# Rounded output products in the first block, and another order of the last mixer's gate chunks

## The chip, the core and the metric

The kernel is one program on one core of a Trainium2 chip. The metric is the device time of one execution in microseconds (us), as the median of some executions. The engines have queues of their own that run in program order: TensorE (PE, matrix products), VectorE (DVE), ScalarE (ACT), GpSimd (POOL), and SyncE (SP), which starts the weight transfers. They wait for one another through semaphores.

## What is computed

Two small transformer stacks, one after the other, over 256 latent tokens of width 1024 (and 256 context tokens in the first layer). Only the parts that the change touches are shown.

```python
# first block, layer 0: pooling beside a gated scan, then one output product
o = rmsnorm(o_sum, onorm_g).reshape(Bn, Ln, HG_WIDTH).astype(g.dtype) * jax.nn.silu(g)
return jnp.concatenate([multiscale_pool(u, pool_w, pool_scale), o], axis=-1) @ w_out
...
x = x + g1 * rmsnorm(y_lat, norm_g[l, 1])
f_lat = swiglu(rmsnorm(x, norm_g[l, 2]) * (1.0 + sc2) + sh2, ffn_w_in[l], ffn_w_out[l])
...
# second block, last mixer (mixer 3): gated delta rule, z is its output gate
lmat = jnp.where(strict, jnp.einsum('nbhid,nbhjd->nbhij', kb, k) * decay, 0.0)
amat = lmat + jnp.eye(CHUNK, dtype=f32)
u = lax.linalg.triangular_solve(amat, v * beta[..., None], left_side=True, lower=True, unit_diagonal=True)
...
o = (o * jax.nn.silu(z.astype(jnp.float32))).astype(x.dtype)
return o.reshape(b, s, C_WIDTH) @ w_out
```

## The kernel before

All weights come as one stream of chunks of 1 MB (128 partitions x 2048 float32) into a ring of six slots; SP loads a slot again once PE has signalled that its chunk is multiplied. The order of the stages is a fixed list, and the order of the work on each engine is the order in which its function is written.

**Split products.** Nearly all products are made from rounded numbers. ACT rounds a chunk into a place of its own (the high part, L494), DVE writes the difference over the ring slot (the low part, L500), and PE adds three products: high by high, high by low, low by high. Inputs are split in the same way (`X_HI` by ACT, `X_LO` by DVE at L521). A product from unsplit float32 numbers is one instruction in the program and two records in the trace.

**The tail of the first mixer (mixer 0).** PE mixes the four heads (L871) into banks 0 to 3 and sums their squares (L876); ACT makes the inverse roots (L953, L955); DVE scales each head out of its bank and multiplies it by its gate (L1077, L1080). Then comes the output product for 4 tiles (2 blocks of 128 tokens by 2 halves of 512 features) of each of two streams, latent and context, unsplit, from `pe_tokens` (L656): 16 products of 128x256 a tile. PE's order is: four latent tiles, one context tile, the latent tokens turned back (`pe_turn_tokens`, L673), one context tile, the sum of squares for the next norm (`pe_norm`, L231), two context tiles. DVE and ACT meanwhile take token statistics (`dve_rms_tokens`, L693 to L702; `act_rms_tokens`, L681 to L685), add the turned tokens to the residual (L711), and make the input of the feed-forward (`dve_scale_output`, L624, L627, L521, with ACT's L484). The feed-forward `ffn0_lat` starts with `pe_chunks_as_features_come` (L299): 32 products of the high weights by the high input, 32 of the low weights, 32 by the low input. It waits until the first half of the context tokens has left banks 4 and 5.

**The same pattern twice more.** After mixer 1 (`mix1_post`, then `ffn1_lat`) and after `ffn1_lat` (then `ffn2`, turned by `pe_turn_both`, L1484) tokens are measured, scaled, turned and added, and there PE has nothing to put beside it. In `dve_add_turned` the additions alternate with the low parts of the next input.

**Mixer 3.** PE multiplies 16 chunks; 12 to 15 are the gate z (48 products of 128x256 each, L286 to L288). After z chunk 12 come eight sums of squares over heads (`head_sums`, L2028), four row spreads (`spread`, L2035), then for each of 8 heads four products (`head_products`, L2043, L2046), with z chunks 13 and 14 between them. DVE's chain over the heads is `decays` (L2377 to L2384), `triangles` (L2390, L2391), `query_decays` (L2394) and `rest_of_head` (L2398, L2399); it holds the difference of chunk 15 between heads 1 and 2. Then six levels of a triangular inverse follow. In a level PE makes `product` (L2098) after DVE's mask (L2420), and four `increments3` groups (L2111, L2116), which DVE adds in (L2445, L2449). z chunk 15 is cut in four parts of 12 products (`last_z_part`, L2076 to L2078), one ahead of each of levels 2 to 5.

## Time and profile before

| what | us |
|---|---|
| median of 3 runs | 2217.38 |
| the runs | 2217.25, 2217.38, 2224.48 |
| the profiled execution, own time | 2223.95 |
| its span in the profile | 2222.0 |
| PE busy in the span | 2151.3 (97%) |
| DVE busy | 1401.9 (63%) |
| ACT busy | 986.8 (44%) |
| POOL busy | 173.4 (8%) |

A time in the trace counts from the start of the span. The engine that is nearly always busy is PE, so the reading looks for the some 70 us in which PE stands still, and for stretches in which its granted clock is one half.

### The profile page before, as it was taken

The numbers are of one execution on the slowest core, as the hardware profiler recorded it, in microseconds if no ns is written. First come the engines' busy times: TensorE is split into PE (matmuls) and PEld (weight loads), VectorE is DVE, ScalarE is ACT, GpSimd is POOL, SyncE is SP. The second block draws the span as 40 slices with busy tenths as digits, with TensorE's granted clock in tenths as the row PEclk, the third lists the DMA queues.
The fourth block names the chain that finished last, engine by engine and source line by source line (L and its number), as shares of the span: only waits on it lengthen the run. The fifth ranks groups of instructions, "written<-read, shape, count | busy, mean of one in ns | idle before, by whom it ended". The sixth has DMA issues, their size and how long they took to land. (4 is left out here: it accounts for less than half of the span.)

```text
span 2222.0 us, 32315 instructions
## 1 busy us (share of the span) xinstructions
PE 2151.3 (97%) x13514; PEld 1851.3 (83%) x13514; DVE 1401.9 (63%) x1602; ACT 986.8 (44%) x1114; POOL 173.4 (8%) x94
## 2 busy tenths in 40 slices
PE   6999999999999999999999999999999999999999
PEld 4887788888888857888888898888988897878888
DVE  4367845666766456656665678656665687566665
ACT  3312333444544234444444555445444565254444
POOL 0065600000000000000100011000100012001000
PEclk8999999999999999999999999999999998999999
DMA  8227913455455412355555533555455442124552
GB/s 334 106 100 295 412 74 131 165 191 192 160 189 189 169 72 76 138 192 189 200 189 189 189 133 142 189 189 189 167 191 190 170 166 100 36 91 163 191 192 79
DMA packets 52609, 373.28 MB, mean 168 GB/s; under 512 B 5792, under 2 KB 6816, under 8 KB 7968
## 3 DMA queue, kind: packets, MB, share of 16 engines
q1 hardware_dynamic: 51632, 367.71, 44.9%
q0 software_dynamic: 880, 4.19, 0.5%
q8 instruction: 71, 1.16, 0.2%
q14 instruction: 26, 0.21, 0.0%
HBM read 370.84 MB, written 1.05 MB: 167 GB/s over the span
## 5 line engine op out<-in xcount | busy, mean ns | idle before, releaser
L500 DVE TENSOR_TENSOR ring_r<-ring,AR_r 128x2048 fp32r<-128x2048 f32 x286 | 655.3, 2298 | 267.3 <-ACT AR_r L494 267.1
L494 ACT ACTIVATE AR_r<-ring 128x2048 fp32r<-128x2048 f32 x286 | 545.0, 1911 | 326.2 <-PE PS L397 195.0
L376 PE MATMUL PS<-AR_r 128*128 128x512 f32 x2240 | 533.2, 390 | 0.0
L376 PEld LDWEIGHTS PS<-AR_r 128*128 128x128 f32 x2240 | 415.6, 188 | 83.1
L380 PEld LDWEIGHTS PS<-AR_r,ring_r 128*128 128x128 f32 x2240 | 287.2, 191 | 10.9
L380 PE MATMUL PS<-AR_r,ring_r 128*128 128x256 f32 x2240 | 290.6, 283 | 0.0
L541 ACT ACTIVATE AR<-PS 128x512 f32<-128x512 f32 x140 | 83.7, 598 | 418.6 <-PE PS L380 418.6
L395 PE MATMUL PS<-AR_r 128*128 128x512 f32 x616 | 241.4, 392 | 0.0
L396 PE MATMUL PS<-ring_r,AR_r 128*128 128x512 f32 x616 | 241.1, 391 | 0.0
L397 PE MATMUL PS<-AR_r 128*128 128x512 f32 x616 | 240.4, 390 | 0.0
L397 PEld LDWEIGHTS PS<-AR_r 128*128 128x128 f32 x616 | 116.0, 188 | 24.7
L603 DVE TENSOR_TENSOR AR<-AR,PS 128x512 f32<-128x512 f32 x70 | 48.1, 688 | 138.9 <-ACT AR L541 138.9
L395 PEld LDWEIGHTS PS<-AR_r 128*128 128x128 f32 x616 | 116.4, 189 | 22.4
L396 PEld LDWEIGHTS PS<-ring_r,AR_r 128*128 128x128 f32 x616 | 116.4, 189 | 21.5
L580 DVE TENSOR_TENSOR AR<-AR,PS 128x512 f32<-128x512 f32 x70 | 48.1, 688 | 95.3 <-ACT AR L541 95.3
L286 PE MATMUL PS<-AR_r 128*128 128x256 f32 x352 | 101.6, 289 | 0.7 <-DVE ring_r L500 0.7
L287 PE MATMUL PS<-AR_r 128*128 128x256 f32 x352 | 99.8, 284 | 0.0
L288 PE MATMUL PS<-AR_r,ring_r 128*128 128x256 f32 x352 | 99.7, 283 | 0.0
L299 PE MATMUL PS<-AR_r 128*128 128x256 f32 x640 | 83.3, 287 | 8.0 <-ACT AR_r L484 4.5
L299 PEld LDWEIGHTS PS<-AR_r 128*128 128x128 f32 x640 | 79.4, 193 | 10.8 <-issue 5.1
L1395 POOL TENSOR_SCALAR X<-X 128x512 f32<-128x512 f32 x24 | 47.6, 2000 | 440.5 <-DVE AR_r L521 440.4
L286 PEld LDWEIGHTS PS<-AR_r 128*128 128x128 f32 x352 | 67.7, 192 | 2.8 <-issue 1.8
(394 smaller groups left out, 2927.2 us busy)
## 6 DMA issues: line engine op xcount, KB each, us to landing
ring<-stream SPq DMA_DIRECT2D x346, 1024.0 KB, 4.8
X<-xt SPq DMA_DIRECT2D x1, 2048.0 KB, 9.0
AR<-bias POOLq DMA_DIRECT2D x1, 1536.0 KB, 6.5
AR<-pt POOLq DMA_DIRECT2D x2, 512.0 KB, 4.5
out<-X SPq DMA_DIRECT2D x4, 256.0 KB, 2.1
AR<-invc SPq DMA_DIRECT2D x1, 512.0 KB, 15.3
X<-negl POOLq DMA_DIRECT2D x1, 512.0 KB, 6.3
H<-wax POOLq DMA_DIRECT2D x1, 512.0 KB, 7.2
```

The costliest lines, as they stand in the source:

```text
L286: pe.matmul(o, w_hi, X_HI[:, k, :], start=(k == 0), stop=False)
L287: pe.matmul(o, w_hi, X_LO[:, k, :], start=False, stop=False)
L288: ins = pe.matmul(o, w_lo, X_HI[:, k, :], start=False, stop=(k == DT - 1))
L299: ins = pe.matmul(PS[:, bank, j * T:(j + 1) * T], w, x[:, k, :], start=(first and j == 0), stop=last, skip_group_check=True)
L376: pe.matmul(PS[:, (6, 4)[half] + j, :], block(w_hi_of(tag, i + half), j, k), X_PARTS[:, k, :], start=(k == 0), stop=False, skip_group_chec ...
L380: ins = pe.matmul(PS[:, (6, 4)[half] + j, 0:T], block(RING_R[:, n % SLOTS, :], j, k), X_HI[:, k, :], start=False, stop=(k == DT - 1), skip ...
L395: pe.matmul(o, G_HI[:, d, f, ts], w_hi, start=False, stop=False, skip_group_check=True)
L396: pe.matmul(o, G_HI[:, d, f, ts], w_lo, start=False, stop=False, skip_group_check=True)
L397: ins = pe.matmul(o, G_LO[:, d, f, ts], w_hi, start=False, stop=(last and f == 1), skip_group_check=True)
L494: act.activation(w_hi_of(tag, i), ring[:, n % SLOTS, :], ACT.Identity).then_inc(split_hi, 1)
L500: dve.tensor_tensor(RING_R[:, n % SLOTS, :], ring[:, n % SLOTS, :], w_hi_of(tag, i), ALU.subtract).then_inc(split_lo, 1)
L541: act.activation(out[:, it % 2, :].rearrange("p (j t) -> p j t", j=2), PS[:, bank:bank + 2, T:T2], ACT.Identity).then_inc(ffn_low, 1)
```

## The change

It has five parts.

1. Mixer 0's output product is split like the others: its chunks hold 256 input features by all 1024 outputs (`chunks_out`), ACT rounds four chunks, DVE makes four differences, the inputs are split too (`POOL_HI`, `SQ_R`, `CAT0_LO`), and PE runs chunk by chunk over all four tiles. Its order: four latent chunks, context chunk 0, the turn, context chunks 1 and 2, the norm's sum, context chunk 3.
2. `dve_scale_output` makes its four multiplications by the inverse root first. This is in all five places that use it.
3. Token statistics and turns: `first_early` scales the first token block before the last statistic (context tokens of mixer 0, `ffn1_lat`); `apart` and `pe_turn_both` let PE turn what is ready instead of waiting for all; `dve_add_turned` makes all additions first, and the difference of `ffn2`'s chunk 1 moves behind them.
4. `pe_chunks_as_features_come` waits for the low weights of each of its two chunks apart.
5. In mixer 3, ACT and DVE split chunk 15 ahead of the norms of the heads; z chunk 13 is cut in two halves, z chunk 15 goes whole between the products of heads 5 and 6, and the level loop holds no z part. PE waits for ACT's logarithms instead of the exponentials before it writes those banks again.

```diff
-SPLIT_OUTS = ('mix1_out', 'mix2_out', 'mix3_out')
+SPLIT_OUTS = ('mix0_out', 'mix1_out', 'mix2_out', 'mix3_out')
...
             for i in chunks:
                 pe.wait_ge(split_lo, SPLIT_BASE[tag] + i + 1)
-            for k in range(DT):
-                products(k, True, X_HI)
+                for k in range(DT):
+                    products(k, True, X_HI, of=(i,))
...
+            for q in range(GROUPS):
+                dve.tensor_tensor(SQ[:, pair(q), cols], src[:, pair(q)], r, ALU.mult).then_inc(S["scaled"], S.mark("scaled", (tag, q)))
             for q in range(GROUPS + 1):
                 if q < GROUPS:
-                    dve.tensor_tensor(SQ[:, pair(q), cols], src[:, pair(q)], r, ALU.mult).then_inc(S["scaled"], S.mark("scaled", (tag, q)))
                     dve.wait_ge(S["scaled"], S.at("scaled", (tag, q)))
...
+                for k in (*range(4, DT), *range(4)) if apart and t == 0 else range(DT):
+                    if apart and k == 0:
+                        pe.wait_ge(S["normed"], S.at("normed", (tag, t)))
+                    if apart and k == 4:
+                        pe.wait_ge(S["token_high"], S.at("token_high", (tag, t)))
...
+            stats(0, 0)
+            stats(0, 1)
+            gather(0)
+            stats(1, 0)
+            if first_early:
+                scale(0)
+            stats(1, 1)
+            gather(1)
+            if not first_early:
+                scale(0)
+            scale(1)
...
+            if nxt:
+                dve_split_chunk(dve, nxt, 1)
+            dve.wait_ge(order.sem, order.n)
             dve.wait_ge(S["residual"], S.at("residual", (tag, GROUPS - 1)))
+            if nxt:
+                dve_split_input(dve, nxt, X[:, :, c])
...
-            pe_tokens(pe, "mix0_out", ctx, CAT0, 0, 0, 0, 4, False)
+            def out_chunk(i, key):
+
+                if key == lat:
+                    pe.wait_ge(split_lo, SPLIT_BASE["mix0_out"] + i + 1)
+                    pe.wait_ge(S["mixer_low"], S.at("mixer_low", ("mix0", i)))
+                for t in range(2):
+                    for h in range(2):
+                        first = T + t * P if key == lat else t * P
+                        if i == 0 and key == lat:
+                            pe.wait_ge(S["mixer_output"], S.at("mixer_output", ("mix0 taken", 2 * t + h)))
...
+            for i in range(4):
+                out_chunk(i, lat)
+            pe.wait_ge(S["o_rinv"], S.at("o_rinv", HEADS - 1))
+            out_chunk(0, ctx)
             pe_turn_tokens(pe, lat, TOK1[0], LOW)
-            pe_tokens(pe, "mix0_out", ctx, CAT0, 0, 0, 1, 5, False)
+            out_chunk(1, ctx)
+            out_chunk(2, ctx)
             pe_norm(pe, ("ffn0_pre", 0), LAT, 0)
-            for h in range(2):
-                pe_tokens(pe, "mix0_out", ctx, CAT0, 0, 1, h, 6 + h, True)
+            out_chunk(3, ctx)
...
+            act_split_chunk(act, "mix0_out", 2, free=START["mix0_out"])
+            for h in range(HEADS):
+                act.wait_ge(S["mixer_output"], S.at("mixer_output", (0, h)))
+                act.activation(SQ_R[:, h, :], GS[:, h, :], ACT.Identity).then_inc(S["x_hi"], S.mark("x_hi", ("mix0_out", 2 + h)))
+            act_split_chunk(act, "mix0_out", 3, free=START["mix0_out"])
...
+            for i in range(2):
+                dve_split_chunk(dve, "mix0_out", i)
+            dve.wait_ge(S["mixed"], S.at("mixed", HEADS - 1))
+            for q in range(2):
+                dve.wait_ge(S["x_hi"], S.at("x_hi", ("mix0_out", q)))
+                dve.tensor_tensor(CAT0_LO[:, pair(q), :], CAT0[:, pair(q), :], POOL_HI[:, pair(q), :], ALU.subtract).then_inc(
+                    S["mixer_low"], S.mark("mixer_low", ("mix0", q)))
...
-            pe_turn_tokens(pe, "mix1_post", TOK1[0], HIGH)
+            pe_turn_tokens(pe, "mix1_post", TOK1[0], HIGH, apart=True)
...
                     if u < 4:
-                        pe.wait_ge(S["head_rinv"], S.at("head_rinv", ("delta", 4 + j)))
+                        pe.wait_ge(S["head_rinv"], S.at("head_rinv", ("log", 4 + j)))
...
             head_sums((4, 5, 6, 7))
+            z_half(13, 0)
             head_sums((0, 1, 2, 3))
-            for h in range(4):
+            for h in range(2):
                 spread(h)
+            z_half(13, 1)
             for h in range(0, 2):
                 head_products(h)
-            z_chunk(13)
+                spread(h + 2)
...
             for h in range(4, 6):
                 head_products(h)
                 spread(h + 2)
+            z_chunk(15)
             for h in range(6, 8):
                 head_products(h)
...
             for lv in range(INNER):
                 first_bank = 0 if lv else 2
-                if lv >= 2:
-                    last_z_part(lv - 2)
...
             for i in range(1, 13):
-                if i < 12:
-                    act_split_chunk(act, "mix3_in", i + 3)
+                act_split_chunk(act, "mix3_in", i + 3)
...
+            dve_split_chunk(dve, "mix3_in", 15)
             for u in (4, 5, 6, 7, 0, 1, 2, 3):
                 dve.wait_ge(S["head_rinv"], S.at("head_rinv", ("delta", u)))
...
-            for i in range(2):
-                dve_split_chunk(dve, "ffn2", i)
-            dve_rms_tokens(dve, order, "ffn1_lat", 0, LOW, TOK1[0], need_tokens(dve, "ffn1_lat", "ffn1_lat", FFN_LAST))
+            dve_split_chunk(dve, "ffn2", 0)
+            dve_rms_tokens(dve, order, "ffn1_lat", 0, LOW, TOK1[0], need_tokens(dve, "ffn1_lat", "ffn1_lat", FFN_LAST), first_early=True)
```

PE at the end of mixer 0, before: the row of the four head sums, the 80 unsplit products, the turn, and on to the feed-forward (L299).

```order
L876 MATMUL PS<-SQ,CO 128x512 x4
L656 MATMUL PS<-ring,AR 128x256 x80
L673 MATMUL PS<-CO,AR 128x128 x16
L656 MATMUL PS<-ring,AR 128x256 x16
L231 MATMUL PS<-SQ,CO 128x256 x8
L656 MATMUL PS<-ring,AR 128x256 x32
L299 MATMUL PS<-AR_r 128x256 x32
```

And now, around the sum for the norm (L231); the L916 rows are the split products, three terms in turn.

```order
L916 MATMUL PS<-ring_r,SQ_r 128x512
L916 MATMUL PS<-AR_r,H_r 128x512
L231 MATMUL PS<-SQ,CO 128x256 x8
L916 MATMUL PS<-AR_r,SQ_r 128x512
L916 MATMUL PS<-ring_r,SQ_r 128x512
L916 MATMUL PS<-AR_r,H_r 128x512
```

The work behind the norm's sum has gone from 32 unsplit products of 256 columns to one chunk, 24 split products of 512 columns; what stands ahead of it has gone from 96 unsplit products to 168 split ones.

DVE where it makes the feed-forward's input and then takes the context tokens' statistics, before:

```order
L624 TENSOR_TENSOR SQ<-X,RI 128x2x256
L627 TENSOR_SCALAR H<-SQ,GV 128x256 x2
L624 TENSOR_TENSOR SQ<-X,RI 128x2x256
L627 TENSOR_SCALAR H<-SQ,GV 128x256 x2
L521 TENSOR_TENSOR AR_r<-H,AR_r 128x2x256
L624 TENSOR_TENSOR SQ<-X,RI 128x2x256
```

and now:

```order
L623 TENSOR_TENSOR SQ<-X,RI 128x2x256 x4
L628 TENSOR_SCALAR H<-SQ,GV 128x256 x4
L521 TENSOR_TENSOR AR_r<-H,AR_r 128x2x256
L628 TENSOR_SCALAR H<-SQ,GV 128x256 x2
L521 TENSOR_TENSOR AR_r<-H,AR_r 128x2x256
L628 TENSOR_SCALAR H<-SQ,GV 128x256 x2
L521 TENSOR_TENSOR AR_r<-H,AR_r 128x2x256 x2
L697 BN_STATS TMP<-PS 128x6 x2
L702 BN_AGGR TMP<-TMP 128x2
L705 SCALAR_TENSOR_TENSOR TMP<-TMP 128x1
L697 BN_STATS TMP<-PS 128x6
L711 TENSOR_SCALAR AR<-PS,TMP 128x512
```

The four multiplications stand in a row ahead of the rest, and the first block's scaling (L711) has moved ahead of the last statistic.

PE in mixer 3, before, from the last product of z chunk 12 to the first of z chunk 13:

```order
L288 MATMUL PS<-AR_r,ring_r 128x256
L2028 MATMUL PS<-SQ,CO 128x512 x8
L2035 MATMUL PS<-AR,CO 128x512 x4
L2043 MATMUL PS<-AR 128x128 x2
L2046 MATMUL PS<-AR 128x128 x2
L2043 MATMUL PS<-AR 128x128 x2
L2046 MATMUL PS<-AR 128x128 x2
L286 MATMUL PS<-AR_r 128x256
```

and now, from the last product of z chunk 13's second half through heads 0 to 2 (L2114 and L2117 are the head products, L2106 the spreads):

```order
L2129 MATMUL PS<-AR_r,ring_r 128x256
L2114 MATMUL PS<-AR 128x128 x2
L2117 MATMUL PS<-AR 128x128 x2
L2106 MATMUL PS<-AR,CO 128x512
L2114 MATMUL PS<-AR 128x128 x2
L2117 MATMUL PS<-AR 128x128 x2
L2106 MATMUL PS<-AR,CO 128x512
L2114 MATMUL PS<-AR 128x128 x2
L2117 MATMUL PS<-AR 128x128 x2
L2106 MATMUL PS<-AR,CO 128x512
```

z chunk 13 has moved ahead of the head products, and spreads stand between them.

## Rows read from the trace of the kernel before

**Rows 1.** The page, busy time of each engine.

```profile
PE 2151.3 (97%) x13514; PEld 1851.3 (83%) x13514; DVE 1401.9 (63%) x1602; ACT 986.8 (44%) x1114; POOL 173.4 (8%) x94
```

**Rows 2.** Timeline of mixer 1's split output products; then page groups of the weight splits.

```profile
869.79 0.39 PE L1217 MATMUL PS<-AR_r 128*128 128x512 f32 x1
...
878.40 0.39 PE L1217 MATMUL PS<-AR_r,H_r 128*128 128x512 f32 x1
...
L500 DVE TENSOR_TENSOR ring_r<-ring,AR_r 128x2048 fp32r<-128x2048 f32 x286 | 655.3, 2298 | 267.3 <-ACT AR_r L494 267.1
L494 ACT ACTIVATE AR_r<-ring 128x2048 fp32r<-128x2048 f32 x286 | 545.0, 1911 | 326.2 <-PE PS L397 195.0
```

**Rows 3.** Timeline of PE, end of mixer 0: start, duration, instruction, [idle before].

```profile
306.19 31.78 PE L656 MATMUL PS<-ring,AR 128*128 128x256 f32 x146 [0.69 <-DVE AR L1080]
...
346.46 3.62 PE L231 MATMUL PS<-SQ,CO 128*128 128x256 f32 x16
349.92 13.98 PE L656 MATMUL PS<-ring,AR 128*128 128x256 f32 x64
365.85 1.34 PE L299 MATMUL PS<-AR_r 128*128 128x256 f32 x9 [1.95 <-DVE AR L702]
```

**Rows 4.** Timeline of DVE and ACT at the same place.

```profile
300.50 0.75 DVE L1077 SCALAR_TENSOR_TENSOR SQ<-PS,SM,SQ 128x512 f32<-128x512 f32 x1 [11.55 <-ACT SQ L955]
...
351.14 0.69 DVE L624 TENSOR_TENSOR SQ<-X,RI 128x512 f32<-128x512 f32 x1 [8.81 <-ACT RI L461]
...
359.05 1.29 DVE L693 BATCH_NORM_STATS2 TMP<-PS 128x6 f32<-128x512 f32 x2
...
361.43 0.69 ACT L685 ACTIVATE AR<-PS,TMP 128x512 f32<-128x512 f32 x1
```

**Rows 5.** Timeline of PE between mixer 1 and its feed-forward.

```profile
881.63 3.32 PE L673 MATMUL PS<-CO,AR 128*128 128x128 f32 x16 [2.84 <-DVE AR L702]
...
892.38 2.50 PE L299 MATMUL PS<-AR_r 128*128 128x256 f32 x16 [3.02 <-ACT AR_r L484]
...
899.05 5.10 PE L299 MATMUL PS<-AR_r,ring_r 128*128 128x256 f32 x32
903.99 4.00 PE L299 MATMUL PS<-AR_r 128*128 128x256 f32 x32
```

**Rows 6.** Timeline of DVE, then PE, between `ffn1_lat` and `ffn2`.

```profile
1076.69 2.29 DVE L500 TENSOR_TENSOR ring_r<-ring,AR_r 128x2048 fp32r<-128x2048 f32 x1 [1.32 <-ACT AR_r L494]
...
1084.69 1.66 DVE L711 SCALAR_TENSOR_TENSOR X<-PS,GV,X 128x256 f32<-128x256 f32 x4 [0.95 <-PE PS L1484]
...
1094.90 4.00 PE L299 MATMUL PS<-AR_r 128*128 128x256 f32 x32
```

**Rows 7.** Stretches of mixer 3: length, busy times, then granted clock, DMA share, GB/s.

```profile
1866.70:1873.10 6.40, 6.37 (x8) 2.14 (x8) 5.67 (x12) 5.33 (x12) 0.00 (x0) 0.56 0.00 0
...
1887.10:1893.10 6.00, 6.00 (x51) 6.00 (x51) 3.28 (x10) 1.31 (x4) 0.00 (x0) 1.00 0.03 11
...
1906.00:1911.50 5.50, 4.86 (x72) 4.33 (x70) 2.74 (x5) 2.33 (x6) 0.00 (x0) 0.50 0.01 3
```

**Rows 8.** Timeline of DVE over mixer 3's heads, then PE's first level product.

```profile
1866.71 2.50 DVE L2366 SCALAR_TENSOR_TENSOR AR<-AR,SQ 128x512 f32<-128x512 f32 x4 [3.96 <-ACT SQ L2234]
...
1875.29 0.28 DVE L2390 TENSOR_TENSOR AR<-AR,PS 64x128 f32<-64x128 f32 x1 [2.20 <-PE PS L2046]
...
1876.91 2.27 DVE L500 TENSOR_TENSOR ring_r<-ring,AR_r 128x2048 fp32r<-128x2048 f32 x1
...
1894.11 0.28 DVE L2390 TENSOR_TENSOR AR<-AR,PS 64x128 f32<-64x128 f32 x1 [3.56 <-PE PS L2046]
...
1903.58 0.62 PE L2098 MATMUL PS<-CO,SQ 64*64 64x64 f32 x14 [2.87 <-DVE SQ L2420]
```

**Rows 9.** Timeline of mixer 3, level 4: DVE's two masks and PE's product.

```profile
1932.28 1.28 DVE L2420 TENSOR_TENSOR SQ<-AR,X 128x512 f32<-128x512 f32 x2
...
1933.18 2.08 PE L2098 MATMUL PS<-AR,SQ 64*64 64x64 f32 x64
```

143 lines of the change are left out of this document (76 added, 67 removed).

## The prediction

> **What bounds the kernel now.** I read the page's busy times first. PE is busy for 2151.3 of 2222.0 us [rows 1], so what an edit is worth is what it takes off PE's queue, or off the 70.7 us in which PE stands still. Next I read the timeline of PE for its idle gaps in the places that the diff touches, then the timelines of DVE and ACT there, for what ends each gap. Last came the granted clock of the stretches in mixer 3, since an idle PE is often followed by a stretch at the lower of the two levels. In the rows the reader should look for three kinds of place: PE full (the output products of mixer 0), PE waiting for a chain through DVE and ACT (the two joints around `ffn1_lat`, the heads of mixer 3), and PE filled with other work just as long as such a chain (the levels of mixer 3).
>
> **Mixer 0: the products.** The unsplit products cost 31.78 us for 146 records, that is 73 products at 0.435 us each [rows 3]. Split products of 512 columns start 38 intervals in 878.40 - 869.79 us, 0.227 us apart [rows 2]. A stream has 64 unsplit or 96 split products, so 27.9 us become 21.8 us.
>
> **Mixer 0: up to the norm.** Ahead of the norm's sum PE had the latent products and two context tiles, 96 x 0.435 = 41.8 us. Now it has 168 x 0.227 = 38.1 us, 3.7 us less. The latent products also stopped for the scaled heads before: one stop of 0.69 us stands in front of 306.19 [rows 3], and with the short ones at their start I count 1.5 us. Now the first chunk needs only the pooled half and the emptied banks. A tile is 6 x 0.227 = 1.36 us, about the pace at which DVE empties the banks, so little of this wait comes back. The norm's sum should end 5.2 us earlier, near 344.7 instead of 349.9.
>
> **Mixer 0: what hides the splits.** They add four ACT passes of 1.91 us and four DVE passes of 2.30 us [rows 2], and the parts of the inputs. DVE sits idle for 11.55 us before 300.50 [rows 4]; two of its passes (4.6 us) and the pooled halves (some 2.5 us, an estimate from half a pass each) fit there. The other two come between the heads' scaling and 314 us or so, while PE has latent chunks of 5.4 us to run; the last is wanted only when chunk 3 is due, near 318. I put these at nothing. If the cover were gone, PE would wait for one DVE pass, 2.3 us, up to two.
>
> **Mixer 0: from the norm to the feed-forward.** Here the bound changes hands. Before, 14.0 us of PE work and a stop of 1.95 us followed the norm's sum, 15.9 us in all [rows 3]. Now PE has only one chunk, 5.4 us, and then waits for DVE. DVE begins the modulation 1.2 us after the sum, is done after 7.9 us (351.14 to 359.05), and the first block's tokens are ready 3.1 us later (361.43 + 0.69 against 359.05), provided that the scaling no longer queues behind the last statistic, which `first_early` sees to [rows 4]. That makes 12.3 us. The feed-forward starts 5.2 + 3.6 = 8.8 us earlier, with a PE gap of 6.9 us in front instead of 1.95. The four multiplications in a row cost DVE nothing more. A gap that long should cost clock: after 2.87 us of idle PE ran at 0.50 for 5.5 us in mixer 3 [rows 7, 8]. I charge 3 us at half speed, 1.5 us, with bounds 0 and 2.8. Sum: -7.3 us.
>
> **After mixer 1.** PE waits 2.84 us and then turns 16 blocks in 3.32 us, at half clock [rows 5]; DVE's additions need ten of them. With `apart`, eight are done in the gap and two after it, so the additions start some 1.8 us earlier. Then the feed-forward's first 32 products follow the high input. They take from 892.38 to 899.05, 6.7 us, because the input comes at DVE's pace; with all multiplications first, ACT alone sets it, four groups at about 1.1 us, then one group of products: 4.3 us. That is 2.4 us more. The next 32 took 5.10 us against 4.00 for the same count at full clock [rows 5], so one stretch of half clock is in this and I leave it in. Sum: -4.2 us, bounds -2 and -5.5.
>
> **Before `ffn2`.** DVE's pass on chunk 1 ends at 1078.98 and only then come the statistics [rows 6], though the first tile's products were done some 2.8 us before. Without that pass, the first statistics start early, the end of the chain is set by the last tile, and the additions start at about 1083.3 instead of 1084.69. Additions in a row give ACT the high input sooner. Chunk 1's difference then ends near 1088.9, in time for its low weights because part 4 lets chunk 0's go first. The last 32 products start near 1092.8 instead of 1094.90. Sum: -2.1 us, bounds 0 and -3.
>
> **Mixer 3: the heads.** DVE's chain from the head norms to the first mask is what PE waits for at 1903.58 (2.87 us idle) [rows 8]. Three delays leave it. The last head norms come 1.3 us earlier: PE no longer idles between the two groups of sums, which gives 1.9 us and more at full clock, less the rounding of chunk 15 that now stands ahead of them on ACT. The wait of 2.20 us for the first head's product goes, since DVE finds it done. The difference of chunk 15, 2.27 us, leaves the middle of the chain for a place where DVE is idle. One delay grows: DVE waited 3.56 us behind z chunk 14; now it waits about 1 us behind chunk 14 and 3.4 us behind chunk 15, each 6.0 us of PE work [rows 7]. Sum: -1.3 - 2.2 - 2.3 + 0.9 = -4.9, and head 7's tail some -0.4: -5.3 us.
>
> **Mixer 3: the levels.** The four z parts are 6 us of PE work, but they cover a DVE chain of the same length. In level 4 the first mask is ready at half of 1.28 us after 1932.28, that is 1932.92; PE's product starts at 1933.18 [rows 9]. Without the part it could start 0.15 us sooner. So four levels give back 0.6 us, not 6, and PE idles about 1.5 us in each. Sum of mixer 3: -5.9 us, bounds -9 (half-clock stretches at 1866.7 and 1906 gone as well) and +2.
>
> **A rule that speaks against this.** The rows show half clock after an idle of 2.87 us [rows 7, 8]. The Trainium skill, TensorE: Matmul & The Clock Gate, section "Why this matters for your kernels", says to leave no idle gaps between bursts, or the clock drops; section "A second HAM failure mode: psum-queue depth-cycling" adds that short, frequent gaps can do it too. By that, the new gaps in the levels would be paid for: the second rival.
>
> **The sum.** -7.3 - 4.2 - 2.1 - 5.9 = -19.5 us. Against the profiled execution, 2223.95 us, this gives 2204.4. The median is 6.6 us under that execution. Some 1.5 us of my gains are the ends of half-clock stretches that a shorter run may not have, so I take 18 us from the median: 2217.4 - 18 = **2199 us**.
>
> **The rivals.**
> *More clock comes back.* PE's work in the heads is closed up, and its two slow stretches, 6.4 us at 0.56 and 5.5 us at 0.50 [rows 7], may both go, and the new gap of 6.9 us may cost nothing. Each slow stretch is worth about half its length where PE sets the pace, so some 6 us more: 2193.
> *The clock falls in the levels (this ends slower).* Place: levels 2 to 5 and z chunks 14 and 15. For: the idle of 1.5 us in each level is new. Against: level 4 is dense with products for the other 5.8 us, at full clock today. Price: a level at half clock takes 11.5 us instead of 7.4, so four cost 16.5 us; the two z chunks at half clock add 12 us less the DVE slack of some 4 us. It decides from about 36 us more at half clock; all of it gives 2199 + 16.5 + 8 = 2224. In part, two levels, it gives 2207.
> *The first mixer's gain is lost on DVE.* If the splits come late or ACT's passes push the head sums, PE stands at each latent chunk and the 5.2 us before the norm go, while the part behind it stays: 2204.
> *The mixer 3 edit does nothing*, because z chunk 15 in front of heads 6 and 7 costs all that the rest gives: 2205.
>
> **How the numbers follow.** Forecast 0.58 (2195 to 2203). More clock 0.13. Clock falls in part 0.10 (2207), in full 0.03 (2224). First mixer lost 0.09, mixer 3 nothing 0.07. The range reaches from 2190 to 2208. A measurement of this kernel tells about 0.5%, 11 us, from no change, so the border is 2206.3. Faster: 0.58 + 0.13 + 0.09 + 0.05 = 0.85; same 0.12; slower 0.03.
>
> **What the changed profile would show.** Behind the norm's sum one group of 24 products, then a PE gap of 6 to 7 us ended by the scaled context tokens: right; a gap among the latent chunks ended by the low parts: the third case. At the start of `ffn1_lat`, 32 products in about 4.3 us. In mixer 3, DVE waits of about 1 and 3.4 us for the products of heads 4 and 6, the first level product 5 us nearer to z chunk 12 than the 50 us of today, and levels of 7.2 us with 1.5 us of idle PE. A granted clock of 0.5 inside the levels would make me wrong, and so would a feed-forward gap after mixer 0 of 2 us or less, which would mean that DVE's chain was not the bound.

## The result

| what | us |
|---|---|
| before, median of 5 runs | 2217.38 (2216.87 to 2224.48) |
| after, median of 5 runs | 2207.47 (2206.83 to 2210.52) |
| after over before | 0.9946, 95% interval 0.9932 to 0.9961 |
| the profiled executions, spans | 2222.0 and 2208.7 |

The changed kernel is 9.9 us faster by the medians and 13.3 us by the two profiles. The forecast was 18 us by the medians and 19.5 by the profiles. So the sign was right, the time lies inside the range at its upper end, and a third (profiles) to nearly a half (medians) of the gain is missing. The prediction took 11 us for what a comparison can tell from no change; the interval here is some 3 us to either side, and it excludes no change.

PE on the changed kernel's page, beside [rows 1]:

```profile
PE 2134.8 (97%) x13450; PEld 1836.4 (83%) x13450; DVE 1412.5 (64%) x1612; ACT 997.7 (45%) x1124; POOL 177.3 (8%) x94
```

PE works 16.5 us less, and stands still 3.2 us more. To see where, I put the start of the same product of both traces side by side. Each step of the distance belongs to the code between two lines of the table; the last column is a second profile of the changed kernel (e10_after_again) against its first.

| milestone on PE | before | after | after - before | second - first |
|---|---|---|---|---|
| first conditioning product | 64.39 | 65.25 | +0.86 | +1.73 |
| mixer 0's output products | 302.08 | 303.07 | +0.99 | -0.80 |
| end of the norm's sum | 350.08 | 346.72 | -3.36 | -0.80 |
| `ffn0_lat`, first input product | 365.85 | 358.41 | -7.44 | -0.80 |
| end of its 96 input products | 377.62 | 372.22 | -5.40 | -0.78 |
| its second step | 403.02 | 396.07 | -6.95 | -0.83 |
| `ffn0_ctx`, second step | 593.12 | 587.79 | -5.33 | -0.87 |
| norm's sum behind mixer 1 | 885.63 | 878.20 | -7.43 | -0.86 |
| `ffn1_lat`, end of input products | 907.99 | 898.21 | -9.78 | -0.87 |
| `ffn2`, end of input products | 1098.90 | 1087.61 | -11.29 | -0.89 |
| `ffn2`, first step | 1100.40 | 1090.66 | -9.74 | -1.00 |
| mixer 3, first product | 1771.38 | 1761.62 | -9.76 | +0.22 |
| mixer 3, first level product | 1903.58 | 1892.57 | -11.01 | -0.72 |
| mixer 3, output products | 1972.71 | 1959.36 | -13.35 | -0.74 |
| last feed-forward, first step | 2013.29 | 2000.06 | -13.23 | -0.73 |

The last column shows how far such a ledger can be trusted. From mixer 0 to `ffn2` two executions of one kernel keep their distance within 0.2 us. They part in front of mixer 0, where nothing was changed, by 2.5 us; by 1.2 us where the second execution had a stretch at the lower clock (1352 to 1356) and the first had none; and by 0.9 us among the heads of mixer 3, where the first one's stretch was longer.

**Mixer 0**, to be held against [rows 3] and [rows 4]. The timeline of PE and DVE of the changed kernel:

```profile
343.10 3.62 PE L231 MATMUL PS<-SQ,CO 128*128 128x256 f32 x16
...
351.78 0.39 PE L916 MATMUL PS<-AR_r,H_r 128*128 128x512 f32 x1
358.41 1.86 PE L299 MATMUL PS<-AR_r 128*128 128x256 f32 x7 [6.24 <-DVE AR L711]
...
347.81 2.50 DVE L623 TENSOR_TENSOR SQ<-X,RI 128x512 f32<-128x512 f32 x4 [12.86 <-ACT RI L461]
```

PE has one group of 24 split products (L916) behind the norm's sum and then a gap of 6.24 us, which DVE's scaling of the context tokens ends. DVE had stood idle for 12.86 us when its modulation (the scaling that makes the feed-forward's input) began. What the gap costs behind it stands in the windows of the 96 input products, after first, then before; the column behind the busy times is the granted clock:

```profile
358.40:364.00 5.60, 5.59 (x29) 5.59 (x30) 3.16 (x5) 4.42 (x6) 0.00 (x0) 0.58 0.01 3
364.00:372.20 8.20, 8.20 (x71) 8.20 (x70) 0.87 (x1) 0.23 (x2) 0.00 (x0) 1.00 0.00 0
```

```profile
365.80:371.40 5.60, 5.55 (x46) 5.56 (x47) 2.97 (x2) 3.90 (x4) 0.00 (x0) 1.00 0.38 159
...
```

The products take 13.81 us instead of 11.77: 2.04 us went to the lower of the two levels (1.2 GHz).

**`ffn1_lat`**, beside [rows 5]. PE of the changed kernel:

```profile
873.34 0.66 PE L677 MATMUL PS<-CO,AR 128*128 128x128 f32 x4
875.44 1.78 PE L677 MATMUL PS<-CO,AR 128*128 128x128 f32 x12 [1.44 <-DVE AR L711]
878.20 3.72 PE L231 MATMUL PS<-SQ,CO 128*128 128x256 f32 x16 [0.98 <-ACT SQ L468]
884.97 5.56 PE L299 MATMUL PS<-AR_r 128*128 128x256 f32 x32 [3.06 <-ACT AR_r L484]
890.37 4.00 PE L299 MATMUL PS<-AR_r,ring_r 128*128 128x256 f32 x32
```

Four turns fill the gap, twelve follow it, and the first 32 input products come without a stop. They take 5.40 us and not the 4.3 forecast, since the half-clock stretch, which lay in the second group of 32 before (5.10 us), now lies in the first. Before, the 16 turns ran at half clock as well (3.32 us, granted clock 0.58 from 881.60 to 885.00); now they run at full clock. So this joint has one such stretch where it had two.

**`ffn2`**, beside [rows 6]. PE, DVE and GpSimd of the changed kernel, the GpSimd row once for all four scalings and once for the first alone:

```profile
1083.61 4.00 PE L299 MATMUL PS<-AR_r 128*128 128x256 f32 x32
1087.45 1.12 PE L1457 MATMUL PS<-CO,X 128*128 128x128 f32 x6
1089.59 1.31 PE L1457 MATMUL PS<-CO,X 128*128 128x128 f32 x10 [1.02 <-POOL X L1464]
...
1079.11 2.49 DVE L521 TENSOR_TENSOR AR_r<-X,AR_r 128x512 fp32r<-128x512 f32 x4
1081.52 2.29 DVE L500 TENSOR_TENSOR ring_r<-ring,AR_r 128x2048 fp32r<-128x2048 f32 x1
...
1079.89 9.64 POOL L1464 TENSOR_SCALAR X<-X 128x512 f32<-128x512 f32 x4 [1.49 <-DVE AR_r L521]
...
1079.89 5.27 POOL L1464 TENSOR_SCALAR X<-X 128x512 f32<-128x512 f32 x1 [1.49 <-DVE AR_r L521]
```

The same scalings in the kernel before:

```profile
1090.72 7.69 POOL L1395 TENSOR_SCALAR X<-X 128x512 f32<-128x512 f32 x4
...
1090.72 1.52 POOL L1395 TENSOR_SCALAR X<-X 128x512 f32<-128x512 f32 x1
```

Behind the 96 products PE turns the residual, which GpSimd scales before. The products end 1.5 us earlier against the end of `ffn1_lat` (-9.78 to -11.29), and PE then waits for GpSimd until the distance is back at -9.74. GpSimd's first scaling took 5.27 us instead of 1.52: it ended 1.35 us after DVE's last pass.

**Mixer 3**, beside [rows 7 to 9]. Windows of the changed kernel (heads 2 and 3; z chunk 14; z chunk 15; the levels), then DVE and PE:

```profile
1866.30:1870.30 4.00, 3.96 (x10) 2.27 (x10) 3.80 (x12) 0.66 (x2) 0.00 (x0) 0.50 0.01 4
1870.30:1878.30 8.00, 8.00 (x50) 7.98 (x50) 3.67 (x11) 1.32 (x4) 0.00 (x0) 0.70 0.00 1
1882.40:1888.40 6.00, 6.00 (x50) 5.94 (x50) 3.37 (x10) 1.32 (x4) 0.00 (x0) 1.00 0.02 8
1892.50:1960.00 67.50, 56.46 (x1207) 51.96 (x1208) 38.66 (x56) 30.96 (x51) 0.61 (x1) 1.00 0.04 11
```

```profile
1879.45 0.28 DVE L2457 TENSOR_TENSOR AR<-AR,PS 64x128 f32<-64x128 f32 x1 [5.29 <-PE PS L2117]
...
1889.48 0.28 DVE L2457 TENSOR_TENSOR AR<-AR,PS 64x128 f32<-64x128 f32 x1 [3.55 <-PE PS L2117]
...
1892.57 1.11 PE L2169 MATMUL PS<-CO,SQ 64*64 64x64 f32 x31 [1.87 <-DVE SQ L2485]
...
1912.79 2.08 PE L2169 MATMUL PS<-AR,SQ 64*64 64x64 f32 x64 [1.39 <-DVE SQ L2485]
...
1919.99 1.21 PE L2169 MATMUL PS<-AR,SQ 64*64 64x64 f32 x34 [1.39 <-DVE SQ L2485]
```

A half-clock stretch (1864.9 to 1875.2) covers the products of heads 2 and 3 and a part of z chunk 14, so that the chunk takes 8 us, and DVE waits 5.29 us behind it. It is no accident of one execution: all ten profiles of the changed kernel and its variants that have chunk 14 whole behind head 3 show half clock in it. Behind chunk 15 DVE waits 3.55 us. A level now takes 7.20 us with an idle PE of 1.39 us, all of it at full clock.

### The profile page after: what moved, and what is told of

Its sections match the earlier page's. It is cut to its first block and busy times, and to the rows that moved or that the text cites. A ratio compares the mean times of both kernels' runs of the same rounds, so it can differ in the third digit from the quotient of the medians.

```text
span 2208.7 us, 32199 instructions
## 1 busy us (share of the span) xinstructions
PE 2134.8 (97%) x13450; PEld 1836.4 (83%) x13450; DVE 1412.5 (64%) x1612; ACT 997.7 (45%) x1124; POOL 177.3 (8%) x94
## 5 line engine op out<-in xcount | busy, mean ns | idle before, releaser
L500 DVE TENSOR_TENSOR ring_r<-ring,AR_r 128x2048 fp32r<-128x2048 f32 x290 | 664.6, 2299 | 264.8 <-ACT AR_r L494 264.5
L494 ACT ACTIVATE AR_r<-ring 128x2048 fp32r<-128x2048 f32 x290 | 553.1, 1913 | 327.5 <-PE PS L397 195.7
L299 PE MATMUL PS<-AR_r 128*128 128x256 f32 x640 | 85.9, 295 | 10.4 <-DVE AR L711 6.2
L299 PEld LDWEIGHTS PS<-AR_r 128*128 128x128 f32 x640 | 83.2, 203 | 12.1 <-DVE AR L711 6.7
```

The lines of the kernel that those rows point to most:

```text
L299: ins = pe.matmul(PS[:, bank, j * T:(j + 1) * T], w, x[:, k, :], start=(first and j == 0), stop=last, skip_group_check=True)
L494: act.activation(w_hi_of(tag, i), ring[:, n % SLOTS, :], ACT.Identity).then_inc(split_hi, 1)
L500: dve.tensor_tensor(RING_R[:, n % SLOTS, :], ring[:, n % SLOTS, :], w_hi_of(tag, i), ALU.subtract).then_inc(split_lo, 1)
```

## The experiments

All start from the changed kernel. Times are medians; the ratio is to the kernel before, run on the same chip in turn. The medians of before lay between 2220 and 2223 us on these chips, so ratios are to be compared, and single places by the milestones.

| run | median | ratio | 95% interval |
|---|---|---|---|
| e1_no_mix0 | 2214.1 | 0.9972 | 0.9956 to 0.9988 |
| e2_norm_early | 2202.95 | 0.9922 | 0.9898 to 0.9947 |
| e3_pool_first | 2207.09 | 0.9929 | 0.9907 to 0.9952 |
| e4_z15_levels | 2204.48 | 0.9920 | 0.9898 to 0.9942 |
| e5_interleaved | 2209.66 | 0.9947 | 0.9930 to 0.9963 |
| e6_not_apart | 2209.04 | 0.9949 | 0.9932 to 0.9965 |
| e7_z14_quarters | 2201.06 | 0.9907 | 0.9890 to 0.9923 |
| e8_three | 2193.88 | 0.9884 | 0.9866 to 0.9903 |
| e9_ffn2_undone | 2209.7 | 0.9950 | 0.9928 to 0.9972 |
| e10_after_again | 2209.48 | 0.9953 | 0.9937 to 0.9968 |
| e11_filler | 2205.45 | 0.9929 | 0.9905 to 0.9954 |
| e12_three_filled | 2188.79 | 0.9858 | 0.9837 to 0.9879 |

### What the split products of mixer 0 are worth

The four chunks, their splits and PE's order are those of before:

```diff
-            for i in range(4):
-                out_chunk(i, lat)
...
+            for t in range(2):
+                for h in range(2):
+                    pe_tokens(pe, "mix0_out", lat, CAT0, T, t, h, 2 * t + h, False, heads_ready if (t, h) == (0, 0) else ())
```

> The changed kernel with the first mixer's output products unsplit again (its four chunks, splits and the order of before), all the rest of the change kept. Theory (the ledger of the two traces): the split products are worth 4.4 us up to the norm's sum and 4.1 us from there to the feed-forward, and pay 2.0 us back as a half-clock stretch behind the 6.24 us gap; so this kernel should take about 6 us more than the changed one, 2213.5, with the feed-forward starting some 15 us behind the start of the norm's sum plus its 3.6 us, a PE gap of 2 us or less in front, and 11.8 us for its first 96 products instead of 13.8. Rival (the gain of this mixer is small, the shorter run comes from the other parts): 2209 or less.

The ratio is 0.0026 (some 6 us) above that of the changed kernel's first comparison, and 0.0019 (some 4 us) above that of its second (e10_after_again). By the milestones it is 73.3 us from the start of the output products to the end of the 96 input products against 69.2, so 4.2 us: the split is worth less than the 6 us of the theory, though not nothing. PE's timeline:

```profile
348.82 13.98 PE L657 MATMUL PS<-ring,AR 128*128 128x256 f32 x64
362.45 4.18 PE L299 MATMUL PS<-AR_r 128*128 128x256 f32 x32
```

The stop of 1.95 us in front of the feed-forward [rows 3] is gone without the split products; the earlier scaling of the first tokens and the other order of the multiplications do that alone. So the parts of this place share the gain: from the norm's sum to the feed-forward 2.3 us come from those and 1.8 from the split, where the theory had given all 4.1 to the split.

### Filling the gap behind mixer 0: earlier work, or no work at all

```diff
             out_chunk(1, ctx)
-            out_chunk(2, ctx)
             pe_norm(pe, ("ffn0_pre", 0), LAT, 0)
+            out_chunk(2, ctx)
             out_chunk(3, ctx)
```

> The changed kernel with the norm's sum one chunk earlier in mixer 0: latent tokens turned, context chunk 1, the norm, context chunks 2 and 3. Theory (behind the norm's sum DVE's chain is the bound, and it is idle for 12.86 us before): DVE's modulation then runs beside chunks 2 and 3, the last statistic follows the last product, and the feed-forward starts about 2.7 us after that product instead of 6.24, 3.6 us earlier; with the shorter gap the half-clock stretch (2.0 us) may go too. 2202 with it gone, 2204 with it left. Rival (the chain behind the last product is as long wherever the norm stands): 2207.5. Rival (the modulation beside the products is slowed or the norm's sum itself stops PE for the squares): slower, 2209.

```profile
335.93 3.62 PE L231 MATMUL PS<-SQ,CO 128*128 128x256 f32 x16
...
351.24 4.08 PE L299 MATMUL PS<-AR_r 128*128 128x256 f32 x32 [0.80 <-DVE AR L711]
```

The gap falls from 6.24 to 0.80 us, more than expected, since DVE takes the context statistics tile by tile as PE ends them. Counted from the output products' start (301.38 here), the feed-forward starts 5.5 us earlier, a whole chunk, and its products run at full clock (another 2.0 us). Of these 7.5 us 5.9 are left at the norm's sum behind mixer 1: a half-clock stretch (382 to 385) now follows the gap of 1.0 us inside `ffn0_lat`, where the changed kernel had none. The two rivals are out. The second run leaves the gap as long as it is and only keeps PE busy in it:

```diff
             out_chunk(3, ctx)
+            for _ in range(44):
+                pe.transpose(PS[:, 0, 0:P], IDENT, IDENT)
```

> The changed kernel with 44 transposes of the identity on PE in the gap behind mixer 0's last product, into a PSUM bank that nothing reads before it is written again (they add work and change no result). Theory (the half-clock stretch of the first feed-forward products follows from the idle 6.24 us): PE is kept busy for 5.3 us of it, the 96 input products take 11.8 us instead of 13.8, and the kernel is 2.0 us faster, 2205.5. Rival (the clock falls there whatever the gap holds, or the transposes do not count): 13.8 us and 2207.5.

```profile
348.32 4.96 PE L935 MATMUL PS<-CO 128*128 128x128 f32 x44
354.72 4.08 PE L299 MATMUL PS<-AR_r 128*128 128x256 f32 x32 [1.44 <-DVE AR L711]
```

```profile
354.70:366.40 11.70, 11.68 (x97) 11.68 (x98) 4.04 (x5) 4.59 (x7) 0.00 (x0) 1.00 0.01 1
383.00:391.00 8.00, 7.16 (x28) 5.89 (x29) 3.96 (x4) 7.34 (x9) 0.00 (x0) 0.79 0.07 30
```

The 96 products take 11.8 us, as they did before the change, and the milestone behind them moves by 2.03 us against the changed kernel's. The idle PE and not something in the code caused the half clock here: all eight profiles that leave this gap of over 6 us open have a half-clock stretch in the products behind it, and the six in which it is filled or short have none. The Trainium skill, TensorE: Matmul & The Clock Gate, section "Why this matters for your kernels", asks that PE not be left idle for long between bursts of products. The first of the two windows agrees; the second, which is read below, shows half clock behind a far shorter gap.

What the 44 useless transposes give to the whole kernel is another question. The second window lies behind the gap of 1.0 us inside `ffn0_lat`. There this profile has a half-clock stretch of 1.6 us cost, and the changed kernel has none, so that at the norm's sum behind mixer 1 only 0.4 us of the 2.03 are left; from the output products to the end of the kernel it is 0.9 us. The medians differ by 2 to 4 us; what gave the rest is not shown. This is what e12_three_filled tests further down: whether the next gaps have to be filled too.

### The modulation's order and the turns after mixer 1

```diff
-            for q in range(GROUPS):
-                dve.tensor_tensor(SQ[:, pair(q), cols], src[:, pair(q)], r, ALU.mult)...
             for q in range(GROUPS + 1):
                 if q < GROUPS:
+                    dve.tensor_tensor(SQ[:, pair(q), cols], src[:, pair(q)], r, ALU.mult)...
```

> The changed kernel with the modulation's multiplications between its gains and shifts again, one group at a time, as before. Theory (the high input came at DVE's pace, now at ScalarE's): from the start of the first feed-forward product to the end of the 96 input products of ffn1_lat 15.6 us instead of 13.2, 2.4 us more in all, 2210. Rival (those 2.4 us between the two traces were a half-clock stretch that fell elsewhere): still 13.2 us at full clock, 2207.5.

```profile
885.26 4.98 PE L299 MATMUL PS<-AR_r 128*128 128x256 f32 x24 [3.06 <-ACT AR_r L484]
890.49 1.22 PE L299 MATMUL PS<-AR_r 128*128 128x256 f32 x8 [0.25 <-ACT AR_r L484]
```

> The changed kernel with the turns after mixer 1 waiting for all four token halves again, as before. Theory (eight turns in the gap let DVE's additions start 1.8 us earlier): 1.8 to 2.1 us more from the end of mixer 1's products to the norm's sum of ffn1, 2209.5. Rival (the turns were not what the additions waited for): 2207.5.

```profile
872.62 3.29 PE L677 MATMUL PS<-CO,AR 128*128 128x128 f32 x16 [2.87 <-DVE AR L711]
...
883.39 4.07 PE L299 MATMUL PS<-AR_r 128*128 128x256 f32 x32 [3.06 <-ACT AR_r L484]
```

Neither is told from the changed kernel by its whole time; the milestones tell. Without `apart` the norm's sum comes 2.17 us later, as expected. But in that profile the half clock fell on the turns (3.29 us for 16) and the products behind ran free, 3.91 us for the first 32; the changed kernel's took 5.40 with half clock in them. At the end of the 96 products `apart` is therefore worth 0.7 us and not 2.1. With the multiplications interleaved the input products take 0.9 us more and not 2.4. Neither theory nor rival was right by itself: where the half clock lies in the first group, PE is slow enough for DVE's pace and hides the order; before, it lay in the second group and was paid beside DVE's stops. That reading of the difference between 0.9 and 2.4 is an argument from where the stretches lie; no run puts them back where they were.

### GpSimd in front of `ffn2`

```diff
             dve_add_turned(dve, order, "ffn1_lat", TURN_BANKS, LAYER1 + G_FFNOUT, 0, "ffn2")
+            dve.wait_ge(S["x_scaled"], S.at("x_scaled", ("ffn2", 3)))
             dve_split_chunk(dve, "ffn2", 2)
```

> The changed kernel, but DVE waits for GpSimd's four scalings of the residual before it takes the low part of chunk 2 of ffn2. Theory (GpSimd makes no headway while DVE works through its passes: its first scaling took 5.3 us beside them, the three others 1.5 us each): the four scalings end near 1087.5 instead of 1089.5, PE's residual turns find them done, and the 1.3 to 1.5 us that this place lost comes back: 2206.1. Rival (GpSimd is slow there for another reason): the four still take 9.6 us, 2207.5. Rival (the low part of chunk 2 is then late for the first low products of the feed-forward): 2208.5.

```profile
1081.07 7.43 POOL L1464 TENSOR_SCALAR X<-X 128x512 f32<-128x512 f32 x4 [1.49 <-DVE AR_r L521]
...
1088.59 1.91 PE L1457 MATMUL PS<-CO,X 128*128 128x128 f32 x16
1090.97 1.42 PE L376 MATMUL PS<-AR_r 128*128 128x512 f32 x5 [0.47 <-DVE ring_r L500]
```

Without the pass on chunk 2 beside them the scalings take 7.43 us instead of 9.64, and PE turns all 16 blocks without a stop. All of the difference is in the first one, 3.07 us instead of 5.27; it still runs beside DVE's low input. The three others take 1.5 us each in both kernels. Of the expected 1.3 us 0.84 arrived; the rest went to a new stop of 0.47 us, in which PE waits for DVE's late pass. The second run undoes this part (`dve_add_turned`, the place of chunk 1's difference and `first_early` as before):

> The changed kernel with the DVE order between ffn1_lat and ffn2 of before: the low part of chunk 1 ahead of the statistics, the first token's scaling behind both, the low input group by group behind each addition; the waits per chunk and the earlier turns stay. Theory (what this part gave in front of the products, 1.3 us, was lost behind them to GpSimd's late scalings): from the end of ffn1_lat's last step to ffn2's first up product the same 33.1 us within 0.3, GpSimd's four scalings near 7.7 us instead of 9.6, 2207.5 in all. Rival (the part is worth the 2.1 us forecast and something else ate it): 2209.5.

```profile
1080.29 7.69 POOL L1464 TENSOR_SCALAR X<-X 128x512 f32<-128x512 f32 x4
```

The input products end 1.5 us later against the changed kernel (-0.66 to +0.86), and the first step starts where it did (-0.69): the part gains 1.5 us and gives all of it back. The Trainium skill, SBUF — State Buffer, section "Who interferes with whom", says that a DVE instruction with two SBUF inputs contends with a GpSimd instruction that reads SBUF, for a shared pair of ports that only one of them holds at a time. The rows agree, and show more: GpSimd did not get in between DVE's passes either. It began at 1079.89 and ended 1.35 us after the last of them (1083.81), and a scaling takes 1.5 us alone, so it made hardly any headway until then.

### The last gate chunk, and the clock among the heads

The chunk goes back into the levels, the rest of the part stays:

```diff
-            z_chunk(15)
             for h in range(6, 8):
                 head_products(h)
...
+                if lv >= 2:
+                    last_z_part(lv - 2)
```

> The changed kernel with the last gate chunk of mixer 3 back in four parts in front of levels 2 to 5, as before; the earlier split of chunk 15, the halves of chunk 13 and the earlier sums are kept. Theory (the whole chunk costs DVE a wait of 3.55 us among the heads, and each level is only 0.17 us shorter without its part): the first level product 3 us earlier, four levels 0.17 us longer each, 2.6 to 2.9 us less in all, 2204.7. Rival (the place of the chunk is what keeps the clock up in the levels): the half-clock stretch of before comes back behind the first level, 2207.5 to 2208.

```profile
1886.62 3.45 PE L2184 MATMUL PS<-CO,SQ 64*64 64x64 f32 x64 [2.87 <-DVE SQ L2502]
```

From the first product of mixer 3 to the first level product it is 127.1 us against 131.0 in the changed kernel, and the way from there to the output products is 67.8 against 66.8. Sum: 2.8 us less, as expected. So the stated core of part 5, the whole chunk between the heads, is what costs, and the rest of the part carries its gain. The rival was half right as well: behind an idle of 2.87 us the first level product runs at half clock again (3.45 us). But that costs nothing here, because the second level's product waits for DVE: it starts 4.22 us behind the first, against 4.23 in the changed kernel.

```diff
-            z_chunk(14)
-            for h in range(4, 6):
+            for h in range(2, 6):
                 head_products(h)
                 spread(h + 2)
+                z_quarter(h - 2)
```

> As e4_z15_levels (the last gate chunk in the levels), and gate chunk 14 cut into four quarters of 1.5 us, one behind each of the heads 2 to 5 instead of whole between heads 3 and 4. Theory (the clock falls at the small PE gaps of 0.3 to 0.9 us between the heads, and the whole chunk then runs at half clock, 8 us, in front of what DVE waits for): with the quarters in those gaps PE stays full, the clock holds, DVE's wait of 5.1 us for head 4 goes to 1 us or less, and the first level product comes 4 us earlier: 2200.5. Rival (the clock falls here whatever fills the gaps): the wait is spread over four heads, half clock remains, gain 2 us: 2202.5. Rival (DVE waits for a quarter at each head): no gain, 2204.5.

The profiled execution was the slowest of five (2212.95, the others 2199.16 to 2202.62), and its window over the heads shows why; below it the same code in e8_three:

```profile
1864.00:1890.00 26.00, 25.44 (x91) 18.77 (x91) 16.06 (x47) 5.79 (x18) 0.00 (x0) 0.54 0.01 2
```

```profile
1855.00:1875.00 20.00, 16.85 (x108) 12.94 (x108) 18.97 (x57) 8.10 (x25) 0.00 (x0) 1.00 0.15 54
```

At full clock the quarters do what the theory said: DVE is busy for 18.97 of 20 us. At half clock PE becomes the bound, and then it stays at half clock for some 24 us. From mixer 3's first product to the first level product it is 132.6 us here against 121.9 in e8_three, which is most of the distance to the other executions. The median is the theory's; that one execution in five is 12 us slower is a price that it had not named.

### Together

> The norm's sum one chunk earlier (as e2_norm_early), the last gate chunk in the levels and chunk 14 in quarters (as e7_z14_quarters), and DVE waiting for GpSimd before the low part of chunk 2 of ffn2 (as e3_pool_first), all on the changed kernel. Theory (the places are apart and add up): 7.5 us at mixer 0, 3 to 7 at mixer 3, 0.8 at ffn2, less a stretch or two at half clock that come elsewhere: 2194 to 2197. Rival (each gain at a joint is met by a new half-clock stretch at another): 2200 or more.

The places add up: 2193.88, 1.2% faster than before. Mixer 3 alone gives 12.0 us from its first product to its output products, where the change gave 3.6. Then more of the gaps are filled with transposes:

```diff
+        def pe_fill(pe, bank, n):
+            for _ in range(n):
+                pe.transpose(PS[:, bank, 0:P], IDENT, IDENT)
```

> As e8_three, with identity transposes on PE in four more of its gaps (they add work and change no result): 8 each in the gaps of 1.0 us behind the norm's sum inside ffn0_lat and ffn0_ctx, 24 in the gap of 3.1 us in front of ffn1_lat, 22 in the gap of 2.9 us in front of mixer 3's first level product. Theory (a half-clock stretch follows an idle of PE, as e11_filler is to show for the one behind mixer 0): the stretches at 380, 572, 876 and 1876 of the e8_three profile, worth 1.4 to 1.7 us each, stay away, that behind ffn2 (1344) stays: 2188 to 2190. Rival (short gaps of 1 us have nothing to do with it, so the two stretches at 380 and 572 stay): 2191. Rival (the stretches come at the next joint instead): 2194.

```profile
869.04 4.10 PE L303 MATMUL PS<-AR_r 128*128 128x256 f32 x32 [0.43 <-ACT AR_r L488]
...
1864.19 2.56 PE L227 MATMUL PS<-CO 128*128 128x128 f32 x22
1867.83 2.21 PE L2201 MATMUL PS<-CO,SQ 64*64 64x64 f32 x64 [1.08 <-DVE SQ L2519]
...
1872.15 1.05 PE L2201 MATMUL PS<-AR,SQ 64*64 64x64 f32 x29 [1.52 <-DVE AR L2535]
```

The windows over the norm's sum inside `ffn0_lat`, the start of `ffn1_lat` and the first level, here and then in e8_three (the line left out is `ffn0_ctx`, with the same 1.00 and 0.79):

```profile
378.00:386.00 8.00, 8.00 (x39) 6.71 (x38) 6.84 (x7) 5.84 (x5) 0.00 (x0) 1.00 0.34 124
...
868.00:876.00 8.00, 7.57 (x64) 7.36 (x63) 8.00 (x16) 7.14 (x11) 0.00 (x0) 1.00 0.00 1
1867.80:1880.00 12.20, 10.65 (x274) 10.01 (x275) 8.43 (x15) 4.66 (x12) 0.00 (x0) 1.00 0.01 3
```

```profile
380.00:388.00 8.00, 8.00 (x32) 6.56 (x32) 5.07 (x6) 6.25 (x8) 0.00 (x0) 0.79 0.00 1
...
876.00:884.00 8.00, 7.35 (x50) 7.38 (x51) 8.00 (x15) 6.75 (x11) 0.00 (x0) 0.79 0.01 3
1876.00:1884.00 8.00, 7.62 (x178) 6.90 (x175) 4.96 (x10) 4.67 (x12) 0.00 (x0) 0.79 0.02 4
```

All four stretches are gone in this profile, also the two behind gaps of 1.0 us. Against e8_three that gave 1.6 us at each of the first two and 1.3 at `ffn1_lat`, but nothing in front of the levels: the second level's product starts 4.32 us behind the first here (row 1872.15) and 4.22 in e8_three, since it waits for DVE at either clock. At 2188.79 us this is the fastest kernel of the case, 1.4% below before. In its profile a stretch at half clock is left at the turns of `ffn2` (1056) and one in the heads (1844 to 1852), where e8_three had none, so a part of the rival that they come elsewhere holds; they cost 0.9 and 2.9 us. And the stretch behind `ffn2` (1344), which no transposes guard and which the theory left in place, stayed away too. So one profile doesn't tell a filled gap from luck; that a stretch is gone at all four filled places at once is the evidence.

### The control

> The changed kernel itself, beside the others on one chip, for a second profile of it. Theory (the instructions of a joint take the same time in every execution, and only the half-clock stretches behind its PE gaps come or stay away): all milestones at equal distance to the first profile's except at such stretches, 2207.5. Rival (the distances between milestones differ elsewhere too, so the ledger of two profiles does not tell single microseconds): differences of over 0.5 us at places without a half-clock stretch.

The last column of the table of milestones is this run. The theory holds from mixer 0 on: two changes of over 0.2 us, 1.2 and 0.9, each at a half-clock stretch. Among the heads the second execution's stretch begins only behind the products of head 3, and DVE then waits 4.35 us behind chunk 14 and not 5.29. The theory does not hold in front of mixer 0. There, in code that no kernel here changes, five profiles of the changed kernel and its near variants (after, e3, e9, e10, e11) reach the output products between 299.4 and 304.3 us.

## Why the prediction came out as it did

Against the two profiles, step by step:

| step | predicted | measured |
|---|---|---|
| mixer 0 up to the norm's sum | -5.2 | -4.35 |
| from there to the feed-forward | -3.6 | -4.08 |
| half clock behind the gap | +1.5 | +2.04 |
| other half-clock stretches up to mixer 1 | 0 | +0.07 |
| turns after mixer 1 | -1.8 | -2.10 |
| input products of `ffn1_lat` | -2.4 | -2.35 |
| `ffn1_lat` to `ffn2` | -2.1 | +0.04 |
| mixer 3, heads | -5.3 | -1.25 |
| mixer 3, levels | -0.6 | -2.34 |
| start of the program, end of the program | 0 | +1.1 |
| sum | -19.5 | -13.2 |

**Mixer 0: right.** DVE's chain is the bound behind the norm's sum, the gap was 6.24 us for 6.9 forecast, and the latent products did not wait for their splits. The 0.85 us missing in front of the norm's sum are the stops of before: 1.5 us were counted, and the 44.4 us from the first output product to the norm's sum hold 0.9 us beside the products and turns. The half clock behind the gap was inside its bounds (0 and 2.8). e2_norm_early shows that the gap came from starting DVE's chain late, behind the place of the norm, and not from its length. The ledger gives this place to the split products; e1_no_mix0 gives 2.3 of the 4.1 us behind the norm to the order of DVE's work.

**After mixer 1: right in the sum**, by 0.25 us, and in part by luck. "With `apart`, eight are done in the gap and two after it" failed: four are done there, because the other four of the first block come behind a wait for DVE's scaling, which stands behind the last statistic here. The step came out near all the same because the turns now run at full clock, where 16 of them at half clock had taken 3.32 us. That the stretch of half clock "is in this and I leave it in" was luck in its place: it moved from the second group of products to the first. Undone one at a time, the two edits are worth 0.7 us (e6_not_apart) and 0.9 us (e5_interleaved) at the end of the input products; the rest of the 4.45 us belongs to the two together and to the second stretch of half clock, which went. No run separates these two.

**Before `ffn2`: wrong**, and the step that failed is that the account ended with the last input product. The forecast of that product was near (1.5 us for 2.1), but PE's next work, the residual's turns, hangs on GpSimd's scalings, and these on DVE being done. The change packed DVE's passes together in front of them. e9_ffn2_undone shows that the gain is returned to the last tenth of a microsecond, and e3_pool_first that DVE's passes are why: with one of them (2.29 us) moved away, GpSimd's first scaling is 2.2 us shorter.

**Mixer 3, heads: the term was mis-sized**, at "one delay grows". The wait behind chunk 15 was 3.55 us (3.4 forecast), but the one behind chunk 14 was 5.29 instead of 1. I let PE run at full clock there; the stretch at half clock, which I had counted as gone only in the rival with more clock, came from 1864.9 to 1875.2 and took 1.9 us from the products of heads 2 and 3 and 2.1 from the chunk, both ahead of what DVE waited for. That makes 4.0 of the 4.3 us by which this wait was too long. The other terms nearly cancel: the head norms came 1.9 us earlier instead of 1.3, and the 0.4 us of head 7's tail did not come. e8_three, at full clock in this place, gives the forecast gain and more, but with the chunks in another order, so it is no test of the clock alone.

**Mixer 3, levels: right in mechanism** (7.20 us a level, 1.39 us idle, no half clock), too small in size, since the half-clock stretch in front of them in the profile before (1906.0 to 1911.5, [rows 7]) stayed away: 4 x 0.17 is 0.7, and the other 1.6 us are that stretch. Four profiles bear this out. They have the z parts in the levels like the kernel before, but hardly any half clock from the second level's product on, and they take 67.5 to 67.8 us for this way (e4, e7, e8, e12) against 69.1 before and 66.8 in the changed kernel.

**From the sum to the median.** The profiles are 13.4 us apart by their own times and the medians 9.9. The profiled execution of before was 6.6 us above its median and that of after 3.1, so the profile of before overstates what was to be won. I took off 1.5 us for this; 3.5 was the number. In the start of the program alone the profiles differ by some 5 us.

Of the rivals, none came true as written. The range held the result by the width given to "the first mixer lost" and "the mixer 3 edit does nothing", and the real loss was a little of each kind elsewhere.

## What to carry to other kernels

When an edit shortens a stretch, follow the account past its last instruction to the next engine that joins, here GpSimd: a gain counts only at the milestone where all waits meet again. Put the sum of squares, or any other short product that starts a long chain on another engine, as early as its inputs allow, and the products that depend on nothing behind it. Where a gap on PE can't be filled with work, transposes into a free bank that end before the awaited data come cost nothing, and at the five places where they were tried the clock was up (one profile each). Whether that saves time is to be read at a later milestone: in e11_filler most of it was lost again at the next gap left open, and in front of the levels the clock was not what the next product waited for.

## What the hardware did that I had not expected

- Half clock was seen behind gaps on PE as short as 1.0 us, and not with eight transposes in them (e12_three_filled; one profile, and such a stretch sometimes stays away by itself). A stretch cost 1.3 to 2.0 us where PE set the pace (1.6 us behind the gaps of 1.0 us), and nothing in the first level, where DVE did.
- The same instructions behind the same gap ran at half clock in one execution and not in another (1352 to 1356 in e10_after_again, none there in the first profile). In e7_z14_quarters it once lasted some 24 us where the pace of PE and DVE was nearly equal.
- GpSimd made hardly any headway under four DVE instructions in a row, 3.9 us, and not only under the one that it met.
